# Table chunks beside the gates: activations side by side in 512 columns, halves added on GpSimd

## The reference, cut to what matters

```python
def peer_ffn(h, w_q, sub_keys, u_tab, v_tab):          # h: 256 tokens x 1024
    q = (h @ w_q).reshape(B, S, PEER_HEADS, 2, PEER_DQ // 2)
    scores = jnp.einsum('bshpd,hpkd->bshpk', q, sub_keys)
...
    ids = jnp.take_along_axis(cand_id, top_pos, axis=-1)   # 16 of 16384 experts a head
    gate = jax.nn.softmax(top_s, axis=-1)
...
        act = jax.nn.gelu(jnp.einsum('thkd,td->thk', u_tab[idx], hx))
        return jnp.einsum('thk,thkd->td', g * act, v_tab[idx])
```

## Time and profile before

| what | us |
|---|---|
| median of 3 runs | 2325.12 |
| lowest and highest of the 3 | 2325.05, 2329.89 |
| the profiled execution's own time | 2328.37 |
| its span in the trace | 2326.7 |
| stretch beside the gates, layer 0 | 861 to 1032 |
| stretch beside the gates, layer 1 | 1795 to 1966 |
| mean granted clock of TensorE | 0.994 of full |

### The profile page before, as it was taken

The page is one execution under the profiler, slowest core; times in us unless marked ns, Lnnn a source line. Parts: engine busy times, 40 slices in busy tenths (PEclk is TensorE's granted clock), DMA queues, the critical chain, the costliest instruction groups (busy, mean ns, idle before and its releaser), DMA issues. The chain is left out here.

```text
span 2326.7 us, 44077 instructions
## 1 busy us (share of the span) xinstructions
PE 2252.8 (97%) x14364; PEld 1893.8 (81%) x14364; DVE 1719.0 (74%) x3192; ACT 1281.5 (55%) x2128; POOL 441.1 (19%) x446
## 2 busy tenths in 40 slices
PE   7989989999999999999999999899999999999998
PEld 7657757975888889998888888488888999888886
DVE  6765775763688888877776776768888887666777
ACT  5544544744476665554545455646666555454454
POOL 0000000000022320015333430002233001333553
PEclk9999999999999999999999999999999999999999
DMA  8555555654477775567777785456777556877775
GB/s 248 176 205 165 171 226 165 253 218 181 155 227 235 235 222 188 185 203 246 240 242 240 241 266 219 154 177 218 233 233 229 187 186 207 247 240 241 243 239 173
DMA packets 248438, 497.90 MB, mean 214 GB/s; under 512 B 58616, under 2 KB 134648, under 8 KB 245008
## 3 DMA queue, kind: packets, MB, share of 16 engines
q1 hardware_dynamic: 248192, 496.29, 66.2%
q10 hardware_dynamic: 144, 0.26, 0.0%
HBM read 461.82 MB, written 34.65 MB: 213 GB/s over the span
## 5 line engine op out<-in xcount | busy, mean ns | idle before, releaser
L3103 PE MATMUL psum<-split_operands 128*128 128x512 f32 x3024 | 687.7, 389 | 0.1
L3103 PEld LDWEIGHTS psum<-split_operands 128*128 128x128 f32 x3024 | 567.5, 188 | 118.6 <-ACT split_operands L3045 0.9
L3082 DVE TENSOR_TENSOR split_operands<-weights_ring,split_operands 128x1024 fp32r<-128x1024 f32 x250 | 308.0, 1232 | 195.6 <-ACT split_operands L3045 195.5
L3045 ACT CAST split_operands<-weights_ring 128x1024 fp32r<-128x1024 f32 x252 | 264.7, 1050 | 330.4 <-PE psum L3103 329.2
L2840 DVE TENSOR_TENSOR split_operands<-weights_ring,split_operands 128x1024 fp32r<-128x1024 f32 x254 | 310.5, 1222 | 91.5 <-ACT split_operands L2757 90.8
L3029 POOL TENSOR_TENSOR arena<-arena,residual_gates 128x256 f32 (+1 forms) x254 | 286.6, 1129 | 394.8 <-DMA residual_gates<-expert_activations 388.9
L2687 PE MATMUL psum<-split_operands 128*128 128x512 f32 x1280 | 321.3, 393 | 2.8 <-ACT split_operands L2757 1.8
L2672 POOL TENSOR_TENSOR wide_sums<-wide_sums 128x256 f32<-128x256 f32 x160 | 133.8, 836 | 782.5 <-ACT wide_sums L2776 782.5
L2757 ACT CAST split_operands<-weights_ring 128x1024 fp32r<-128x1024 f32 x254 | 267.2, 1052 | 4.3 <-DMA weights_ring<-in_hg_w_in_dram 2.1
L2687 PEld LDWEIGHTS psum<-split_operands 128*128 128x128 f32 x1280 | 230.1, 189 | 45.0 <-ACT split_operands L2757 2.3
L393 PEld LDWEIGHTS psum<-split_operands 128*128 128x128 f32 x1728 | 208.3, 192 | 6.7 <-DVE split_operands L409 2.8
(11 more groups left out here) (355 smaller groups left out, 2886.1 us busy)
## 6 DMA issues: line engine op xcount, KB each, us to landing
weights_ring<-in_peer_u_dram SPq DMA_DIRECT2D x256, 512.0 KB, 3.5
weights_ring<-in_peer_v_dram SPq DMA_DIRECT2D x256, 512.0 KB, 4.5
expert_activations<-residual_gates SPq DMA_DIRECT2D x256, 128.0 KB, 1.9
residual_gates<-expert_activations SPq DMA_DIRECT2D x256, 128.0 KB, 4.1
split_words<-in_w_ada_dram SPq DMA_DIRECT2D x20, 768.0 KB, 6.6
arena<-in_w_ada_dram SPq DMA_DIRECT2D x12, 1024.0 KB, 6.9
weights_ring<-in_w_in_dram SPq DMA_DIRECT2D x10, 1024.0 KB, 7.3
weights_ring<-in_hg_w_in_dram SPq DMA_DIRECT2D x10, 1024.0 KB, 7.1
```

What stands on the lines that cost most here:

```text
L3045: nc.scalar.copy(self.vs[:, s % 2, 0], self.v[:, s]).then_inc(self.v_high, 1)
L3082: nc.vector.tensor_tensor(self.vs[:, s % 2, 1], self.v[:, s], self.vs[:, s % 2, 0].bitcast(F32), ALU.subtract).then_inc(self.v_low, 1)
L3103: return K.nc.tensor.matmul(K.ps[:, 4 + 2 * t + half], gates[:, w, t * P:(t + 1) * P], v[:, wv, half * 512:(half + 1) * 512], start=(start ...
```

## The change

Chunks 80 to 126 become wide as well; only the last one, 127, stays narrow. TensorE's `chunk_and_gates` calls `wide_products`, ScalarE's takes the gelu of the chunk two before and then copies the chunk before (`follow`), and GpSimd adds the halves of all chunks but the last. The gelu of chunk 126 moves behind the last keeps and the first cast of values. The turn of the loop that holds the last chunk is written out as straight-line code, on every engine.

```diff
--- before.py
+++ after.py
@@ -2491,9 +2491,11 @@
         for u, groups in enumerate(BESIDE):
             body(i * len(BESIDE) + (ROUTED + u), u % SLOTS, [(i * BUILT + o, o) for o in groups], early)
 
+    turns = (NKEYS - ROUTED) // len(BESIDE)
     turn(0, True)
-    with engine.Fori(1, (NKEYS - ROUTED) // len(BESIDE)) as i:
+    with engine.Fori(1, turns - 1) as i:
         turn(i, False)
+    turn(turns - 1, False)
 
 
 SLOTS = 4
@@ -2671,7 +2673,9 @@
                 pool.wait_ge(copied, n + 1)
                 nc.gpsimd.tensor_tensor(wide[:, b, 0], wide[:, b, 0], wide[:, b, 1], ALU.add).then_inc(summed, 1)
 
-            pipeline(pool, 0, ROUTED, SLOTS, add_halves)
+            pipeline(pool, 0, NKEYS - SLOTS, SLOTS, add_halves)
+            for n in range(NKEYS - SLOTS, NKEYS - 1):
+                add_halves(n, n % SLOTS, False)
             pool.wait_ge(K.a_loaded[l][0], 16)
             pool.wait_ge(weights.w_out, GROUPS)
             nc.gpsimd.tensor_tensor(weights.kept[:, 0], weights.kept[:, 0], K.a[:, 0], ALU.mult
@@ -2692,11 +2696,8 @@
                                             start=False, stop=(k == KD - 1), skip_group_check=True)
                 last.then_inc(a_ready, 1)
 
-            def products(n, b, early):
-                if early:
-                    pe.wait_ge(copied, n - 1)
-                else:
-                    pe.wait_ge(gelu_done, n - 1)
+            def products(n, b):
+                pe.wait_ge(copied, n - 1)
                 pe.wait_ge(ut_high, n + 1)
                 for k in range(KD):
                     for wh in range(2):
@@ -2725,13 +2726,14 @@
 
             def chunk_and_gates(n, s, groups, early):
                 first = early and groups[0][1] == 0
-                sooner = early and groups[0][1] in (0, BESIDE[1][0])
                 if first:
-                    products(n, s % 2, sooner)
+                    wide_products(n, s % 2, False)
                 for g, o in groups:
                     weights.pe(pe, g, o % 2, o % 4, early)
-                if not first:
-                    products(n, s % 2, sooner)
+                if isinstance(n, int) and n == NKEYS - 1:
+                    products(n, s % 2)
+                elif not first:
+                    wide_products(n, s % 2, False)
 
             pipeline(pe, 0, SELECT_AT, SLOTS, chunk)
             pe.wait_ge(sel_ready, 1)
@@ -2794,11 +2796,7 @@
             def chunk_and_gates(n, s, groups, early):
                 first, o0 = groups[0]
                 high(n, s, False)
-                if early and o0 == 0:
-                    follow(n, s, False)
-                    wide_gelu(n - 1, (s - 1) % SLOTS, False)
-                else:
-                    gelu(n - 1, (s - 1) % SLOTS, False)
+                follow(n, s, False)
                 for back in range(len(BESIDE[TURN.index(o0) - 1]), 0, -1):
                     if not early or o0 > 0:
                         weights.keep(act, first - back, (o0 - back) % 4)
@@ -2821,6 +2819,7 @@
                 weights.keep(act, g, g % 4)
             act.wait_ge(K.v_loaded[l][0], 16)
             nc.scalar.copy(first_v[:, 0], values[:, 0]).then_inc(first_v_high, 1)
+            wide_gelu(NKEYS - 2, (NKEYS - 2) % SLOTS, False)
             act.wait_ge(first_weighed, 1)
             nc.scalar.copy(first_g[:, 0], weights.kept[:, 0]).then_inc(first_g_high, 1)
             gelu(NKEYS - 1, (NKEYS - 1) % SLOTS, False)
```

## The result

The kernel after takes 2356.86 us in the median of four runs (2354.63 to 2357.58), the kernel before 2325.93 beside it: ratio 1.0128, 95% interval 1.0116 to 1.0140. It is 31 us slower; +41 was forecast (2366 us, with a range of 2345 to 2384).

A forecast was written before the change was run, and what follows sets the result against it. TensorE's 10.59 us and a three-engine loop were taken to bound the 10.60 us turn. 16 turns x 2 layers x (11.85 - 10.60) = 40.0 us plus 1.0 at the stage ends gave +41, 2366 us; range 2345 to 2384.

The forecast's parts named there:

- What bounded the kernel: Beside the gates: TensorE's work of 10.59 us a three-chunk turn and a loop through three engines with 0.07 us slack.
- TensorE's gain: Beside the gates: wide chunk 2.87 us against 2.95, a gain of 0.08; TensorE's turn falls to 10.35 us.
- The adds: GpSimd's 0.75 us adds beside the gates delay VectorE's two-tile instructions, costing 0.33 or 0.56 us each.
- Where the three adds fall: In each turn beside the gates: two adds lengthen the 10.73 us loop by 0.56 each, to 11.85 us.
- The two places named: A, B, C are a turn's chunks: A's add delays C's second compare, B's its second group's product, 0.56 us each.
- the add of C': C' is the previous turn's two-group chunk; its add falls partly in VectorE's wait for the cast, costing the loop nothing.
- The straight-line last turn: Beside the gates: the written-out last turn issues the same instructions in the same order; put at nothing.
- The end of the stage: Behind the gates: chunk 126's later gelu delays SP's store, reload and load; 0 to 2.5 us a layer, 0.5 taken.
- TensorE keeps the pace: Rival, beside the gates: turn of 10.35 us, kernel faster by 8 to 14 us, 2317 or 2311; chance 0.05.
- The adds hide: Rival, beside the gates: only ScalarE's copy counts, turn 10.73 us, +4 us, 2329; chance 0.05.
- Collisions cost less than positioned: Rival, beside the gates: turn is VectorE's 11.41 us of work, +27 us, 2352; chance 0.2.
- the likeliest case: The forecast itself: turns beside the gates of 11.6 to 12.0 us, +33 to +46; chance 0.6.

The follow-up runs named there:

- experiment 8: Kernel before (narrow chunks, no adds) with ScalarE's keeps moved behind the next step's cast and all turns straight-line; 2328.66 us, ratio 1.0010.
- experiment 1: Kernel after without GpSimd's adds beside the gates (gelu of chunks 80 to 126 sees the left half alone); 2330.3 us, ratio 1.0013.
- experiment 6: Kernel after without adds beside the gates (right half left out) and with ScalarE's keeps behind the next step's cast; 2328.45 us, ratio 1.0003.
- experiment 7: Kernel after with the adds beside the gates on VectorE, ScalarE's keeps behind the next cast, all turns straight-line; 2331.24 us, ratio 1.0015.
- experiment 11: Kernel after with adds on VectorE, keeps behind the next cast, straight-line turns and a layer's last three chunks narrow; 2323.06 us, ratio 0.9987.
- experiment 2: Kernel before, narrow chunks kept, plus one spare GpSimd add for each of chunks 80 to 126, result unread; 2351.87 us, ratio 1.0112.
- experiment 3: Kernel after with all four turns of the gates written as straight-line code on every engine; 2346.49 us, ratio 1.0081.
- experiment 5: Kernel after with ScalarE's keeps of a step moved behind the next step's cast, adds still on GpSimd; 2349.77 us, ratio 1.0099.
- experiment 10: Kernel after with a layer's last three chunks narrow and the stage's end in the order of the kernel before; 2351.18 us, ratio 1.0109.
- experiment 12: Adds on VectorE, late keeps, straight-line turns, last three chunks narrow, plus SP's last store ahead of the fourth load of values; 2324.76 us, ratio 0.9983.
- experiment 9: Kernel after with adds on VectorE, late keeps, straight-line turns, and the first chunk of each turn of three narrow; 2328.15 us, ratio 1.0006.

## Why the prediction was right, and where its size was off

*What bounded the kernel.* Right. TensorE's own turn of 10.59 us held it (experiment 8), and a loop of nearly the same length stood beside it: experiment 1 lengthened it by ScalarE's copy to the 10.72 us worked out.

*TensorE's gain.* Right: a wide chunk takes 2.89 us where 2.87 was taken, and TensorE's turn, with nothing in its way, is 10.41 for 10.35 (experiments 6, 7 and 11). So the surplus behind the gates' short matmuls stays (0.09 us where 0.07 was left in); the whole change could not give more than 32 x 0.19 = 6 us.

*The adds.* Right, with the price: 0.97 where 0.42 was, as in the earlier trace rows. The Trainium skill, "SBUF — State Buffer", section "SBUF: two separate sides", explains it by an exclusive lock on shared ports. The traces agree that the one that comes second waits, but it loses some 0.55 us to an add of 0.75, not the whole of it. Experiment 1 takes the adds away and experiment 2 puts them in alone.

*Where the three adds fall.* This is the term that was mis-sized: "Loop: 10.73 + 0.56 + 0.56 = 11.85 us", for all 32 turns. Measured are 11.02 us in the 16 straight ones and 11.69 in the mean of the 16 looped, which alternate between 12.10 and 11.28. The two places named are there in the turn of 12.10. But the sum behind them is not: VectorE was to wait for the cast in every turn, so that the add of C' "costs the loop nothing". In the turn of 12.10 it doesn't wait, and pays for four adds, that of C' (933.24) and that of the B before (928.60) among them. In the other turn it waits 0.38 us and pays 0.31 and 0.56, and B's add hits C's low part instead. I had given that case as the low bound, 11.41, with the loss inside the same turn; in the trace the loss passes to the next turn, and I had looked for one steady turn. In straight-line code VectorE has 9.96 - 0.55 = 9.4 us of work, and three adds at 0.54 make 11.02. The table has 25.3 us in place of 40.0. Experiments 3 and 5 show the parts: without addresses 11.02 everywhere; with the keeps behind the cast 12.10 still, and 10.72 for 11.28. Experiment 2 has the 12.10 with no copy at all, so it is VectorE's turn and not the loop of the forecast.

*The straight-line last turn.* Taken at nothing. It gains: its turns are 0.67 us shorter than looped ones in the mean, since VectorE sets the pace. On the kernel before the same edit gives nothing (experiment 8), because TensorE did.

*The end of the stage.* 0.5 us a layer were taken, from 0 to 2.5; measured are 1.6 and 1.3. The chain was the one described, one step longer: SP issues the fourth load of values just ahead of the last store, the store lands late, the reloads of the output stage wait for it, and TensorE waits for chunk 2. In the kernel after, SP and TensorE in order of time:

```profile
1046.66 0.46 SPq L2664 DMA_DIRECT2D weights_ring<-in_peer_v_dram  x1
1047.25 0.35 SPq L2651 DMA_DIRECT2D expert_activations<-residual_gates  x1
1051.11 0.80 SPq L3009 DMA_DIRECT2D residual_gates<-expert_activations  x2
```

```profile
1051.49 2.88 PE L3102 MATMUL psum<-split_operands 128*128 128x512 f32 x12
1055.28 0.96 PE L3102 MATMUL psum<-split_operands 128*128 128x512 f32 x3 [0.90 <-ACT split_operands L3044]
```

From store to reloads are 3.86 us here; in the kernel before the store was issued at 1032.24 and the reloads at 1033.94. Experiment 10 brings TensorE's wait from 0.90 us down to 0.31, and the output stage is back at 345.8. Experiment 12 takes the wait away in its arrangement, and the output stage stays as long, so this chain is shown for the kernel after and not for the others.

*The rivals.* "TensorE keeps the pace" has its 10.41 us turn only with the adds gone from GpSimd and, in looped code, the keeps behind the cast, and even then the kernel was no faster until the last chunks were narrow too. "The adds hide" is refuted by experiment 2. "Collisions cost less than positioned" (+27) came nearest: the traces differ by 28.9 us, which is below the likeliest case's own +33 to +46, and inside the range only because that rival was in it. It came about by a mixture of turns that none of the cases named.

*Open.* Experiments 7, 9, 11 and 12 give back 1 to 4 us a layer in the output stage, and only part of it is a wait for the reloads. In the trace of 12, the matmuls of its first ten us run some 1.3 us later in sum than before, in both layers, and the cause was not separated. The 3.9 us of experiment 11 in the timed runs stand beside 2.6 us in the two layers of its trace; the interval of its ratio, 0.9 to 5.1 us, holds both. The rest of the 5.2 us between the two traces' spans lies ahead of the gates of either layer, where the kernels are alike: the stretch up to chunk 80 ends anywhere from 857.2 to 864.3 us in these traces.

## What to carry to other kernels

An engine that is idle is not free: ask what it shares with the engine that is nearly full. Three adds of 0.75 us on an idle GpSimd cost VectorE some 1.6 us a turn, more than the 1.0 us (10.95 - 9.96) that they cost when VectorE does them. When a second engine is within a few per cent of the bound, work out its turn in each form of the code (looped and straight) and follow the phases over more than one turn: a collision that falls outside one turn's loop is paid in the next. A gain in a stage is only a gain when its last steps still hand over in time.

## What the runs showed of the hardware

In the rows read here, a VectorE instruction that reads two tiles and a GpSimd add hardly ran side by side: the one that comes second waits, VectorE for some 0.55 us where the add takes 0.75. A VectorE search that reads one tile does run beside an add, in the kernel before:

```profile
1657.20 0.28 DVE L2870 FIND_INDEX8 arena<-arena 128x8 uint32<-128x128 f32 x1
```

```profile
1657.09 0.75 POOL L2672 TENSOR_TENSOR wide_sums<-wide_sums 128x256 f32<-128x256 f32 x1 [2.04 <-ACT wide_sums L2776]
```

Neither is longer than elsewhere (0.75 us for the add in the earlier trace rows). The routing has instructions with two tiles as well, and adds do meet them; what the 160 adds cost there was not measured. And VectorE's register instructions, 57 ns each in the trace, show in the time: 0.11 us at five places of a looped turn, where VectorE sets the pace.
